# A weight remainder made in one GpSimd operation of 1024 elements instead of two of 512

## The reference, cut to what matters

```
u = rms_norm(h, g_mix_pre) @ w_in                      # first block
h = h + rms_norm(concat(attention, recurrence) @ w_out, g_mix_post)
ff = (silu(fn @ w_ffn_gate) * (fn @ w_ffn_up)) @ w_ffn_down
...
u = rms_norm_2(x, norm1_g) @ w_in                      # second block
...
sc = einsum('thcd,hckd->thck', xt @ w_query, sub_keys) # top_k of scores picks experts
u = expert_down[ib]                                    # act = gelu(u . x), out = (gate * act) @ expert_up[ib]
```

## Time and profile before

| | us |
|---|---|
| median of 3 runs (3459.26 to 3461.52) | 3461.25 |
| the profiled execution, its own time | 3463.77 |
| its span | 3462.0 |
| TensorE matmul busy | 3273.0 (95%) |
| GpSimd busy | 2905.4 (84%) |
| ScalarE busy | 1508.1 (44%) |
| VectorE busy | 1079.3 (31%) |

### The profile page before, as it was taken

The page is one execution under the profiler, slowest core; times in us unless marked ns, Lnnn a source line. Parts: engine busy times, 40 slices in busy tenths (PEclk is TensorE's granted clock), DMA queues, the critical chain, the costliest instruction groups (busy, mean ns, idle before and its releaser), DMA issues.

```text
span 3462.0 us, 59974 instructions
## 1 busy us (share of the span) xinstructions
PE 3273.0 (95%) x21000; PEld 2955.1 (85%) x21000; DVE 1079.3 (31%) x1979; ACT 1508.1 (44%) x2006; POOL 2905.4 (84%) x2164
## 2 busy tenths in 40 slices
PE   7978989999999987999799998999999999999999
PEld 7868779999988866777578998999999988888887
DVE  6175132222200032344511264066665111111111
ACT  4734443333334344433334333433333455555554
POOL 6676878899989965898377889877888899999998
PEclk9999999999999999999899999999999999999999
DMA  6434545555555553554245554554445566566665
GB/s 203 154 113 133 173 137 182 183 181 183 182 192 194 192 171 113 170 166 150 79 153 181 173 172 146 184 162 162 163 161 167 193 191 192 193 193 194 193 191 180
DMA packets 159409, 588.40 MB, mean 170 GB/s; under 512 B 17840, under 2 KB 18096, under 8 KB 157904
## 3 DMA queue, kind: packets, MB, share of 16 engines
q1 hardware_dynamic: 156960, 570.50, 50.4%
q10 hardware_dynamic: 2352, 16.55, 1.3%
HBM read 582.78 MB, written 4.19 MB: 170 GB/s over the span
## 4 chain that ended last, share of the span: by engine, by line
PE 82%; DVE 3%; POOL 1%; ACT 1%; issue 1%; ACTq 0%; DVEq 0%; POOLq 0%
PE ps L1622 26%; PE ps L1624 26%; PE ps L1623 26%; PE ps L1685 3%; POOL lo L412 1%; PE ps L1680 1%; DVE hx L1170 1%; ACT xn L457 0%; PE ps L1741 0%; DVE at L1054 0%; DVE at L1066 0%; DVE small L1057 0%; DVE xn L922 0%; DVE xl L926 0%; DVE g L1256 0%
## 5 line engine op out<-in xcount | busy, mean ns | idle before, releaser
L412 POOL TENSOR_TENSOR lo<-raw,hi 128x512 fp32r<-128x512 f32 x2160 | 2905.2, 1359 | 546.3 <-PE ps L1624 322.7
L439 ACT ACTIVATE hi<-raw 128x1024 fp32r<-128x1024 f32 x1080 | 1128.3, 1059 | 1135.2 <-PE ps L1624 737.4
L1622 PE MATMUL ps<-xh,hi 128*128 128x256 f32 x4288 | 1226.2, 286 | 20.1 <-POOL lo L412 13.6
L1623 PE MATMUL ps<-xl,hi 128*128 128x256 f32 x4288 | 1215.4, 283 | 0.0
L1624 PE MATMUL ps<-xh,lo 128*128 128x256 f32 x4288 | 1215.0, 283 | 0.0
L1622 PEld LDWEIGHTS ps<-xh,hi 128*128 128x128 f32 x4288 | 824.9, 192 | 24.4 <-POOL lo L412 13.3
L1623 PEld LDWEIGHTS ps<-xl,hi 128*128 128x128 f32 x4288 | 825.0, 192 | 0.3
L1624 PEld LDWEIGHTS ps<-xh,lo 128*128 128x128 f32 x4288 | 824.9, 192 | 0.0
L1622 PE MATMUL ps<-hi,hg_h 128*128 128x512 f32 x1024 | 399.1, 390 | 3.9 <-POOL lo L412 3.9
L1624 PE MATMUL ps<-hi,hg_l 128*128 128x512 f32 x1024 | 399.0, 390 | 0.0
L1623 PE MATMUL ps<-lo,hg_h 128*128 128x512 f32 x1024 | 398.9, 390 | 0.0
(11 more groups left out here) (276 smaller groups left out, 2443.0 us busy)
## 6 DMA issues: line engine op xcount, KB each, us to landing
raw<-in_stream SPq DMA_DIRECT2D x1080, 512.0 KB, 3.4
gbc<-in_gains ACTq DMA_DIRECT2D x3, 1024.0 KB, 4.7
hx<-in_x SPq DMA_DIRECT2D x2, 1024.0 KB, 7.3
wg<-in_w_gates ACTq DMA_DIRECT2D x1, 2048.0 KB, 7.5
bias<-in_rpb ACTq DMA_DIRECT2D x1, 2048.0 KB, 8.1
w_pr<-in_w_proj ACTq DMA_DIRECT2D x1, 2048.0 KB, 7.7
spill<-hx ACTq DMA_DIRECT2D x1, 2048.0 KB, 7.5
hx_end<-spill ACTq DMA_DIRECT2D x1, 2048.0 KB, 7.9
```

Source lines behind the costliest of these rows:

```text
L412: nc.gpsimd.tensor_tensor(lo[:, k % 2, n], raw[:, k, n], hi[:, k, n].bitcast(F32), ALU.subtract)\
L439: nc.scalar.activation(hi[:, k, :], raw[:, k, :], ACT.Copy).then_inc(hi_done, 1)
L1622: M.matmul(out_ap, a[0], b[0], start=start, stop=False)
L1623: M.matmul(out_ap, a[0], b[1], start=False, stop=False)
```

## The change

GpSimd makes the whole remainder of a piece in one operation of 1024 elements. It waits for `hi_done` and for `unit_used` of the piece two before; the semaphore `half_used` is gone. `lo_done[k]` counts pieces instead of halves, so SP's wait and TensorE's `ready` have new values, and TensorE waits once, ahead of a piece's first matmul, for the whole remainder. TensorE raises one semaphore at a piece's end. The matmuls, their order and the data are the same.

```diff
@@ sync
-                    sp.wait_ge(lo_done[k], i * 2)
+                    sp.wait_ge(lo_done[k], i)
@@ gpsimd
             def take_lo(i, k, first):
                 pool.wait_ge(hi_done, i * 4 + (k + 1))
-                for half, used in enumerate((half_used, unit_used)):
-                    if not (first and k < 2):
-
-                        pool.wait_ge(used, i * 4 + (k - 1))
-                    n = slice(half * NCH, (half + 1) * NCH)
-                    nc.gpsimd.tensor_tensor(lo[:, k % 2, n], raw[:, k, n],
-                                            hi[:, k, n].bitcast(F32), ALU.subtract)\
-                        .then_inc(lo_done[k], 1)
+                if not (first and k < 2):
+
+                    pool.wait_ge(unit_used, i * 4 + (k - 1))
+                nc.gpsimd.tensor_tensor(lo[:, k % 2, :], raw[:, k, :], hi[:, k, :].bitcast(F32),
+                                        ALU.subtract).then_inc(lo_done[k], 1)
@@ tensor
-            def ready(i, k, half):
-                pe.wait_ge(lo_done[k], i * 2 + (half + 1))
+            def ready(i, k):
+                pe.wait_ge(lo_done[k], i + 1)
@@ t_block
-                        if j % 4 == 0:
-                            ready(i, k, j // 4)
+                        if j == 0:
+                            ready(i, k)
...
-                        if j == 3:
-                            ins.then_inc(half_used, 1)
                         if j == 7:
                             ins.then_inc(unit_used, 1)
@@ n_piece
+                ready(i, k)
                 for j in range(2):
-                    ready(i, k, j)
...
-                    ins.then_inc((half_used, unit_used)[j], 1)
+                ins.then_inc(unit_used, 1)
@@ up_piece
+                ready(i + r0, k)
                 for n in range(2):
-                    ready(i + r0, k, n)
...
-                        if tt == 1:
-                            ins.then_inc((half_used, unit_used)[n], 1)
+                ins.then_inc(unit_used, 1)
```

More of the change, by code:

```diff
@@ L172, in build @@
         loaded = [sem(f"loaded{k}") for k in range(4)]
-        hi_done, unit_used, half_used = sem("hi_done"), sem("unit_used"), sem("half_used")
+        hi_done, unit_used = sem("hi_done"), sem("unit_used")
         lo_done = [sem(f"lo_done{k}") for k in range(4)]
```

## The result

The changed kernel is slower by 2.4%: 3543.76 us (median of 4 runs, 3541.11 to 3545.89) against 3461.39 (4 runs, 3459.26 to 3462.77), ratio 1.0239, interval 1.0223 to 1.0255. The direction was forecast, the size was not: +82 us where +26 stood, and 28 us above the range. The profiled execution took 3545.83 us, its span is 3544.0.

What follows compares the result with a forecast made beforehand. TensorE bounds the kernel, GpSimd close behind. Terms 8 + 5 + 7 + 2 + 2 + 2 = +26 on the profiled 3463.8 us gave 3489.8, 3487 us against the runs' median; range 3465 to 3516.

Steps and rivals of the forecast that it cites:

- T = 2.40: GpSimd's remainder operation of 1024 elements: taken to last 2.40 us, ends 2.34 and 2.58.
- the 2.45: Sign of error: a mean of GpSimd's remainder operation above 2.45 us, with the n stages then carrying the loss.
- 0.16 and 0.14: Hand-over from TensorE to GpSimd: 0.16 us tail of the last matmul, then 0.14 us to GpSimd's start.
- The steady term: Undisturbed n pieces: remainder 0.03 us late, TensorE stalls once in two pieces, 8 us in all.
- Steady t pieces, 0: Undisturbed t pieces: 2.88 us a piece leaves slack of 0.13 us, so no cost.
- VectorE's long operations: Stalls behind VectorE's turns at the port: peer_down +5 us, in2 +7 and +2 (kn), first attention +2.
- first attention: Five heads: VectorE's probabilities held up by longer GpSimd operations, +2 us (0 to 6).
- Late starts, +2: Start of peer_up and once in peer_down: where ScalarE's copy is late, TensorE waits 1.1 us longer, +2 us.
- DMA, 0: Transfers into raw: start 1 to 1.3 us later, covered by 3.8 us, no cost; hi waiting for DMA would show error.
- The ring is what costs: Rival, steady pieces: a longer operation costs more, 3509 us with T at 2.48, 3549 at 2.58; chance 0.14.
- The other two: Rivals: fewer turns at the port make it faster, 3444 us, chance 0.06; nothing changes, 3463 us, chance 0.10.
- H: Theory of the experiments: a remainder that misses the weight load's moment costs a slow restart beyond its gap.

Runs made afterwards that it cites:

- e8: Changed kernel with all hi products of a piece run ahead of the first lo product: 3479.74 us, ratio 1.0054.
- e11: e8 with the remainder made in two operations of 512 instead of one of 1024, both after the unit: 3463.66 us, ratio 1.0007.
- e1: Kernel before, only TensorE waits once for the whole piece, GpSimd still makes halves: 3472.26 us, ratio 1.0033.
- e4: Changed kernel with GpSimd's operation over 960 of 1024 elements from the second round on, for timing only: 3496.32 us, ratio 1.0102.
- e10: Changed kernel, in peer_up TensorE waits for the next piece's hl_done in the middle of the piece before: 3535.24 us, ratio 1.0212.

## Why the prediction was wrong in size

Of the 82 us, 64 go with the order of e8 (the kernel after less e8): the steady loss of some 58 and stalls that its longer lead hides. 16 are the longer operation beside VectorE (e8 less e11), and 2 the rest (e11 less before). By the prediction's own steps:

- **T = 2.40: right.** The median in down is 2.402 us (2.342 to 2.414), in peer_up 2.407. From the figure of the Trainium skill ("GPSIMD Engine Reference", Performance versus the Vector engine) for 2048 elements the prediction had an estimate of 2.36; the measurement decides, and with 2.36 the forecast would have been further off. The mean over all 1080 is 2.459, above the 2.45 that I had named as the sign of a T too large; but the mean holds the operations that VectorE held up, so that sign was badly chosen.
- **0.16 and 0.14: right** (1107.99 to 1108.13). So is the gap: 0.02 to 0.04 us ahead of one piece in two in down, where 0.03 stood.
- **The steady term, 8 us: the step that failed.** "From its end to the first matmul, 0.05 us" was taken as the whole price of being late. The number itself holds (0.06), but it comes from a stall of microseconds and tells when a waiting TensorE resumes, not by when the remainder must be there for TensorE to lose nothing. That moment is the weight load, 0.23 us before the matmul, and behind a missed one the piece runs slower by 0.13 to 0.18. In down a late piece costs 0.15 us on average where 0.03 stood (0.22 in the one shown), 8.4/88 = 0.10 per piece over all; in peer_up, with two semaphores, 0.23 per late piece and 32.7/256 = 0.13 per piece. The steady term measures some 58 us instead of 8. The rows to see it were at hand: the weight load of the earlier trace rows's boundary, and the matmul that starts after a stall with a longer record than its neighbours' 0.39 (0.65 in the earlier trace rows, though part of that is the clock).
- **Steady t pieces, 0: right** for query (+0.3 us). Wrong for ffn, +7.7 us or 0.04 a piece: a weight load of this kind is issued 0.12 us ahead of its matmul (before, a load at 599.85 for the matmul at 599.97), which the slack of 0.13 just covers, and once in four pieces a short operation of VectorE stretches the remainder (2.49 us from 594.54). It ended at 597.03, the matmul came 0.15 behind that, at 597.18 instead of 597.11 (a second semaphore, of the bank, is waited for there too), the next two 0.19 and 0.12 later: 0.13 lost on that piece.
- **VectorE's long operations: about right in sum, in in2 not by its working.** Peer_down: its waits for `lo` are 14.8 us against 12.2 before (11.8 of them in the earlier trace rows), and the stage is 4.9 longer, +5 forecast. In in2 the forecast had two stalls of 2.7 a pair; TensorE's rows after have them in pairs, the second smaller:

```profile
1588.61 0.80 PE L1619 MATMUL ps<-hi,xh 128*128 128x512 f32 x1 [2.62 <-POOL lo L410]
1594.06 0.50 PE L1619 MATMUL ps<-hi,xh 128*128 128x512 f32 x1 [1.01 <-POOL lo L410]
1669.90 0.57 PE L1619 MATMUL ps<-hi,xh 128*128 128x512 f32 x1 [2.41 <-POOL lo L410]
1675.35 0.51 PE L1619 MATMUL ps<-hi,xh 128*128 128x512 f32 x1 [0.83 <-POOL lo L410]
```

  6.9 us where 10.8 stood and 5.4 were before, so these stalls grew by 1.5 us and not by 5.4. In2 is 12.8 longer, about 6 of it the steady loss; in e8 it is 6.9 longer, +7 and +2 were forecast. All terms but the steady one summed to 18, and 18 us stay in e8. That the two sums agree is luck: in e8 the start and in1 hold 8.5 of them, where +2 stood for first attention, and peer_down none, where +5 stood.
- **Late starts, +2: right** for peer_up: the wait of 3.89 is 5.0 now.
- **DMA, 0: right.** `hi` waits for the transfer for 815.8 us, which I had named as a sign of error; but GpSimd waits for `hi` in 20 places only (123.4 us), and e8, with the same late transfers (its copy waits as long), is at full pace. A transfer that is waited for by an engine with slack of its own costs nothing.
- **The rivals.** "The ring is what costs" had the right place and, at its 2.58 end, even the time (3549), by a reason that the trace excludes (T was not long). That was luck. The other two are out: no stage with long VectorE operations became shorter, and the time did change.

e1's 12 us, where H had 1 to 6, suggest that the lead itself hid more of VectorE's holds than I had priced.

What stays open: why the restart is spread over a dozen matmuls and not over one. No run here tells. Nor does one place the wait between a weight load and its matmul, which would show whether the price goes when the load alone is let through.

## What to carry to other kernels

Of a TensorE wait ask when the weight load behind it would be issued if nothing were late: the wait must be over then, and once the steady lead falls under that, price a slow restart on every late piece (in down 0.15 us on average where the gap was 0.02), not the gap. A busy share near 100% does not show it; the number of matmuls in a stretch does. Where two engines share a port, keep the operations of the one that has slack short, and give a waiting TensorE the products first that need only what is early.

## What the runs showed of the hardware

- A TensorE stream of 512-column matmuls at 0.227 us distance issues each weight load 0.23 us ahead of its matmul; a load held back to its matmul's start (0.27 late) is followed by distances of 0.34, 0.24, 0.24, 0.23 at a granted clock of 1.00.
- It is the lateness of the load that costs: 0.03 us a piece at 0.02 to 0.15 late (down, after), 0.11 at 0.19 late though its matmul is in time (peer_up, e4), 0.15 at 0.21 to 0.30 late (down, after), 0.23 at 0.33 late (peer_up, after).
- Where two semaphores are waited for at the same place, TensorE's first matmul came 0.14 to 0.15 us after the end of the operation that raises the later one, instead of 0.05 to 0.06; with one of the waits moved away (e10) it was 0.05.
- GpSimd's subtraction of float32 in SBUF takes 2.407, 2.269 and 2.130 us for 1024, 960 and 896 elements per partition: 2.16 ns an element and 0.19 us fixed.
- A VectorE operation of 0.42 us became one of 2.10 us beside GpSimd operations of 2.41, with VectorE's busy time up from 1079 to 1463 us. In e8 peer_up is at full pace all the same: its result has four pieces of room.
